# Where the scale sums of the opening are computed: VectorE alone, or GpSimd and ScalarE

## Chip, cores and metric

The kernel runs on one core of a Trainium2 chip. The metric is the time of one execution on the device in microseconds (us), given as the median of several runs. The profile is of one more execution.

## What is computed

The reference is a decoder trunk of two layers on a residual stream x of 512 tokens by 1024 features (D), with a conditioning vector c. Each layer has a SwiGLU channel mixer at half step, a token mixer (retention in layer 0, a diagonal state space in layer 1) and another channel mixer. What matters here is what stands ahead of the first channel mixer:

```
c_act = silu(c)
sh1, sc1, g1, ... = split(c_act @ ada_w[0] + ada_b[0], 9)
h = modulate(rms_norm(x, norm_g[0, 0]), sh1, sc1)      # y * (1 + sc1) + sh1
x = x + 0.5 * g1 * swiglu_ffn(h, ffn_w_in[0, 0], ffn_w_out[0, 0])
```

A shift sh1 or a scale sc1 is a vector of 1024 numbers, and each of them is the inner product of c_act with one column of ada_w. The change is about the scales.

## The kernel before

Features lie on the 128 partitions, so that x is eight tiles of 128 features by 512 tokens (KT = 8). Matrix products with f32 operands are made from two parts: a high part rounded to fp32r (h_hi, w_hi) and the rest (h_lo, w_lo). Each product of a block is three matmuls: h_hi with w_lo, h_hi with w_hi and h_lo with w_hi. ScalarE writes the high parts, VectorE subtracts to get the low parts (the "splits").

The five engines each run an instruction list in order, and wait for each other by semaphores that the program counts by hand. SP and ScalarE's queue issue the loads of the opening: x, the row of c (spread to all partitions in csil), the first pair of weight chunks in halves, and eight blocks ada_first, one for each tile t of features, 1 MB each. A block holds for its 128 features the weights of the shift (index 0) and of the scale (index 1), 1024 each, along the free dimension.

The shift or scale of a tile is thus a sum along the free dimension of the product of such a block with csil. On VectorE one custom instruction makes the product and the sum at once (the function modulation, L1200, and a short one that reads the accumulator); it starts the sum with the bias from par, where the parameters are kept.

In the opening VectorE works as follows. It sums the squares of x, makes the shift and the scale of tile 0 (first_shift, first_scale) and the first halves of the low parts of two weight chunks (split_first, L1423). Then follows a loop over the tiles t (L1400 to L1458): norm_mult (L1400) multiplies x by the scale and by the reciprocal root that TensorE has spread over a bank of PSUM, first_shift makes the shift of tile t + 1, norm_lo (L1405) makes h_lo of tile t, after t = 1 and 2 a second half split follows, and first_scale makes the scale of tile t + 1 (with L1434, which adds 1 and multiplies by the gain of the norm). ScalarE writes h_hi of tile t (L1166) between norm_mult and norm_lo. TensorE (begin, L2339 to L2343) runs twelve matmuls for each tile, eight with h_hi and four with h_lo, into four banks.

GpSimd makes the reciprocal root of the mean square by a power (norm, L642), waits for a small load dt and makes a second power from it, of 128x64 (L688), whose result is read later for the state space layer. Much later it multiplies and adds on six tiles of the state space layer (s5, L670 and L673), counted by the semaphore us_scaled.

Names of the listing: pool is GpSimd, act ScalarE, dve VectorE, sp the queue of loads, pe TensorE; st counts VectorE's own steps, and st.wait() waits until the last of them is written.

Of the kernel before, what the change touches and what calls it, by code (L numbers as in the profile page):

```python
# [10 lines left out]
ALU = mybir.AluOpType  # L11
ACT = mybir.ActivationFunctionType
# [4 lines left out]
KT = D // P  # L17
TT = L // P
# [70 lines left out]
COL_G = 2 * N_MOD * KT  # L89
# [34 lines left out]
def build(nc, ins, out):  # L124
    pos_d = ins["positions"]
    ctx = ExitStack()
    with ctx:
        def sem(name):
            return ctx.enter_context(nc.semaphore(name))
# [30 lines left out]
        mods = sb("mods", [P, 2 * N_MOD * KT])  # L160
        par = sb("par", [P, N_PAR])
        scale1 = sb("scale1", [P, KT])
# [17 lines left out]
        ada_first = sb("ada_first", [P, KT, 2, D], F32, g_at + HB)  # L180
# [35 lines left out]
        csil = sb("csil", [P, D], F32, tz_at)  # L216
# [74 lines left out]
        def st_slot(q, r):  # L291
            slot, count = ST_SLOTS[q, r]
            return slot, IN0 + count
# [47 lines left out]
        tile_in = [sem(f"tile_in{t}") for t in range(KT)]  # L341
        c_row_in, csil_done, mods_ready = sem("c_row_in"), sem("csil_done"), sem("mods_ready")
# [15 lines left out]
        y_last, scaled_act, scaled_dve = sem("y_last"), sem("scaled_act"), sem("scaled_dve")  # L358
# [26 lines left out]
        us_dve, us_pool, us_scaled = sem("us_dve"), sem("us_pool"), sem("us_scaled")  # L385
        consts_e, zeroed, decays_done = sem("consts_e"), sem("zeroed"), sem("decays_done")
        v_done, v_read, sc_done, y_done, gelu_done = sem("v_done"), sem("v_read"), sem("sc_done"), sem("y_done"), sem("gelu_done")
        a5_hi, a5_lo, gate_done = sem("a5_hi"), sem("a5_lo"), sem("gate_done")

        st_in, st_added = [*x_in, *w_first[0]], sem('st_added')  # L390
        t_summed, t_hi_done, t_lo_done = rot_done, rot_hi_done, rot_lo_done
        st_summed, st_hi_done, st_lo_done, st_used = masked, s_hi_done, s_lo_done, score_done
# [17 lines left out]
        def _(sp):  # L410
# [201 lines left out]
            ffn(3)  # L612
            out_v = out.rearrange("b (t p) n -> p (b t) n", p=P)
            for i in range(TT // 2):
                for scaled, t in ((scaled_dve, i), (scaled_act, TT // 2 + i)):
                    sp.wait_ge(scaled, i + 1)
                    sp.dma_start(out_v[:, t], x_tok[:, t]).then_inc(stored, 16)
            sp.wait_ge(stored, 16 * TT)

# [1 line left out]
        @block.gpsimd  # L621
        def _(pool):
            nc.gpsimd.memset(ident[:], 0.0).then_inc(consts, 1)
            nc.gpsimd.memset(ones[:], 1.0).then_inc(consts, 1)
            nc.gpsimd.memset(mhalf[:], -0.5).then_inc(consts, 1)
            nc.gpsimd.memset(ones_d[:], 1.0 / D).then_inc(consts, 1)

            nc.gpsimd.memset(rho[:], float(np.e)).then_inc(consts_e, 1)
            pool.wait_ge(consts, 4)
            nc.gpsimd.affine_select(out=ident[:], in_=ident[:], compare_op=ALU.not_equal, fill=1.0, base=0,  # L630
                                    pattern=[[-1, P]], channel_multiplier=1).then_inc(consts, 1)

            def norm(k):

                if k in EARLY_AT:
                    pool.wait_ge(early_ms, EARLY_AT[k] + 1)
                    nc.gpsimd.tensor_tensor(rstd[:, 0:2], ms[:, 0:2], mhalf[:, 0:2], ALU.pow).then_inc(early_rstd, 1)
                    pool.wait_ge(ms_done, k + 1)
                    nc.gpsimd.tensor_tensor(rstd[:, 2:4], ms[:, 2:4], mhalf[:, 2:4], ALU.pow).then_inc(rstd_done, 1)
                    return  # L640
                pool.wait_ge(ms_done, k + 1)
                nc.gpsimd.tensor_tensor(rstd[:], ms[:], mhalf[:], ALU.pow).then_inc(rstd_done, 1)  # L642

            def retention():
                with pool.Fori(0, HEADS) as h:
                    for I in range(TT):
                        pool.wait_ge(gn_var, h * TT + (I + 1))
                        nc.gpsimd.tensor_tensor(gn[:, I % 2, 1:2], gn[:, I % 2, 0:1], mhalf[:, 0:1],
                                                ALU.pow).then_inc(gn_rstd, 1)
            def s5():  # L650
                pool.wait_ge(params_in, 32)
                pool.wait_ge(mods_done, MODS_NEED[5])
                pool.wait_ge(xn_done, 4 * KT + 2)
                for t in decays:
                    nc.gpsimd.memset(t[:].rearrange("p (g c) -> p g c", c=NC)[:, :, 0:1], 0.0).then_inc(zeroed, 1)
                for t in (*s_prev, zeros):
                    nc.gpsimd.memset(t[:], 0.0).then_inc(zeroed, 1)

                pool.wait_ge(rb_ready, 1)
                for b in range(US_DVE, KT):  # L660

                    if b == US_DVE:
                        pool.wait_ge(v_done, 1)
                    elif b < 6:
                        pool.wait_ge(sc_done, b - 2)
                    else:
                        pool.wait_ge(a5_lo, (1, 3)[b - 6])
                    v = us[:, b].rearrange("p (g c) -> p g c", c=NC)
                    pool.wait_ge(tile_in[b], 32)
                    nc.gpsimd.tensor_tensor(v, v, spread[:].unsqueeze(1).broadcast_to([P, GB, NC]),  # L670
                                            ALU.mult).then_inc(us_scaled, 1)
                    pool.wait_ge(us_scaled, b - US_DVE + 1)
                    nc.gpsimd.tensor_tensor(v, v, us_shift[:, :, b].unsqueeze(2).broadcast_to([P, GB, NC]),  # L673
                                            ALU.add).then_inc(us_pool, 1)

            def add_blocks(f):
                for q in range(FIRST[f], FIRST[f] + BLOCKS[f]):
                    for k, (r, other) in enumerate(((L_S1, A22), (L_S3, A11))):
                        slot, count = st_slot(q, r)
                        pool.wait_ge(st_in[slot], count)  # L680
                        if q or k:
                            pool.wait_ge(st_added, 32 * q + 16 * k)
                        pool.dma_start(st_block(q, r), ins["w_st"][q, other], accum_op=ALU.add).then_inc(st_added, 16)

            norm(0)
            pool.wait_ge(consts_e, 1)
            pool.wait_ge(dt_in, 16)
            nc.gpsimd.tensor_tensor(dt[:], rho[:], dt[:], ALU.pow).then_inc(exp_done, 1)  # L688
            norm(1)
            retention()  # L690
            norm(2)
            add_blocks(1)
            norm(3)
            norm(4)
            s5()
            norm(5)
            add_blocks(3)
            norm(6)
# [3 lines left out]
        def _(act):  # L702
            st = Steps(act, act_steps)
# [454 lines left out]
            for h in range(2):  # L1158
                r = slice(h * HALF, (h + 1) * HALF)
                for k in range(2):  # L1160
                    act.wait_ge(w_first[k][h], 16)
                    copy(w_hi[k][:, r], w_raw[k][:, r]).then_inc((w_hi_half, w_hi_done)[h], 1)
            for t in range(KT):
                act.wait_ge(mods_ready, t + 1)
                act.wait_ge(xn_done, 1 + t + 1)
                nc.scalar.activation(h_hi[:, t], slots[t % 4], ACT.Identity, bias=mods[:, t:t + 1]).then_inc(h_hi_done, 1)  # L1166
            ffn(0)
            retention()
            out_phase(C_RET_OUT, RET_OUT, OUT_PAIRS * 2, begun=True, early=(2, 6 * KT))
# [10 lines left out]
        def _(dve):  # L1180
            st = Steps(dve, dve_steps)
            V = nc.vector
# [225 lines left out]
            def begin():  # L1408
# [17 lines left out]
                def first_shift(t):  # L1426
                    dve.wait_ge(tile_in[t], 16)
                    modulation(ada_first[:, t, 0], slice(t, t + 1)).then_inc(mods_ready, 1)

                def first_scale(t):  # L1430
                    at = slice(KT + t, KT + t + 1)
                    st(modulation(ada_first[:, t, 1], at))
                    st.wait()
                    st(V.scalar_tensor_tensor(out=scale1[:, t:t + 1], in0=mods[:, at], scalar=1.0,  # L1434
                                              in1=par[:, COL_G + t:COL_G + t + 1], op0=ALU.add, op1=ALU.mult))
                    st.wait()
# [4 lines left out]
                dve.wait_ge(stat_done, 1)  # L1441
                V.tensor_scalar(ms[:], ps[:, 4, 0:TT], 1.0 / D, NORM_EPS, ALU.mult, ALU.add).then_inc(ms_done, 1)
                first_scale(0)
                st(V.memset(acc[:], 0.0))
                for k in range(2):
                    split_first(k, 0)
                dve.wait_ge(rbc_done, 1)
                for t in range(KT):
                    if t >= 4:
                        dve.wait_ge(h_lo_done, t - 3)  # L1450
                    norm_mult(t)
                    if t + 1 < KT:
                        first_shift(t + 1)
                    norm_lo(0, t, 0)
                    if t in (1, 2):
                        split_first(t - 1, 1)
                    if t + 1 < KT:
                        first_scale(t + 1)  # L1458
                dve.sem_inc(mods_done, ADA_FIRST)

            def set_coef(l, s, factor, need):
# [1286 lines left out]
US_DVE = 2  # L2748
# [94 lines left out]
```

## Time and profile before

| what | value |
|---|---|
| median of 3 runs | 2075.45 us (2073.07 to 2076.8) |
| the profiled execution: time, span | 2077.54 us, 2075.7 us |
| granted clock of TensorE, mean | 0.995 |
| busy: TensorE, VectorE, ScalarE, GpSimd | 2023.8, 1316.7, 660.1, 69.1 us |

The span is the stretch from the first to the last recorded work of the profiled execution; its own time is a little longer. Busy time is that in which an engine had an instruction in work, waits excluded. All times of the trace are counted from the start of the span, and the opening is about its first 62 us.

### The profile page before, as it was taken

The numbers are of one execution on the slowest core, as the hardware profiler recorded it, in microseconds if no ns is written. First come the engines' busy times: TensorE is split into PE (matmuls) and PEld (weight loads), VectorE is DVE, ScalarE is ACT, GpSimd is POOL, SyncE is SP. The second block draws the span as 40 slices with busy tenths as digits, with TensorE's granted clock in tenths as the row PEclk, the third lists the DMA queues.
The fourth block names the chain that finished last, engine by engine and source line by source line (L and its number), as shares of the span: only waits on it lengthen the run. The fifth ranks groups of instructions, "written<-read, shape, count | busy, mean of one in ns | idle before, by whom it ended". The sixth has DMA issues, their size and how long they took to land.

```text
span 2075.7 us, 27715 instructions
## 1 busy us (share of the span) xinstructions
PE 2023.8 (97%) x11279; PEld 1770.4 (85%) x11279; DVE 1316.7 (63%) x1841; ACT 660.1 (32%) x777; POOL 69.1 (3%) x81
## 2 busy tenths in 40 slices
PE   4999999999999999999999999999998999999998
PEld 3788888998888889888988988888887898999886
DVE  6677556565455466888865566663548757888522
ACT  2322222333232233223432332322232234444322
POOL 2000000000000000000000000000002000100000
PEclk9999999999999999999999999999999999999999
DMA  8455656433233163666666244453797426666421
GB/s 323 142 197 178 204 189 199 162 115 107 81 106 106 61 226 127 215 222 179 167 233 203 89 159 144 144 172 128 236 320 263 128 82 193 183 178 168 153 97 56
DMA packets 233237, 344.04 MB, mean 166 GB/s; under 512 B 33009, under 2 KB 194033, under 8 KB 230257
## 3 DMA queue, kind: packets, MB, share of 16 engines
q1 hardware_dynamic: 195328, 289.95, 41.7%
q10 hardware_dynamic: 34064, 39.07, 5.4%
q0 software_dynamic: 3744, 13.63, 3.9%
q8 instruction: 70, 1.15, 0.2%
q14 instruction: 31, 0.25, 0.0%
HBM read 315.09 MB, written 31.72 MB: 167 GB/s over the span
## 4 chain that ended last, share of the span: by engine, by line
PE 66%; issue 23%; DVE 7%; DMA 1%; ACT 1%; POOL 0%; ACTq 0%; SPq 0%; POOLq 0%; DVEq 0%
PE ps L2166 16%; PE ps L2167 16%; PE ps L2168 16%; PE ps L2193 5%; PE ps L2194 5%; PE ps L2197 5%; DVE ada_first L1200 1%; DVE w_lo L1190 1%; PE ps L2483 1%; DMA w_raw<-in_ffn_w_out 1%; PE ps L2620 0%; DMA csil<-in_c 0%; DVE tur L1721 0%; DVE h_lo L1247 0%; ACT w_hi L704 0%
## 5 line engine op out<-in xcount | busy, mean ns | idle before, releaser
L704 ACT ACTIVATE w_hi<-w_raw 128x1024 fp32r<-128x1024 f32 (+1 forms) x300 | 294.1, 1026 | 344.7 <-PE ps L2168 239.3
L1190 DVE TENSOR_TENSOR w_lo<-w_raw,w_hi 128x1024 fp32r<-128x1024 f32 x146 | 178.5, 1223 | 275.8 <-ACT w_hi L704 270.8
L2166 PE MATMUL ps<-g_hi,w_lo 128*128 128x512 f32 (+1 forms) x952 | 345.9, 363 | 0.2 <-DVE w_lo L1190 0.2
L2168 PE MATMUL ps<-g_hi,w_hi 128*128 128x512 f32 (+1 forms) x952 | 344.9, 362 | 0.0
L2167 PE MATMUL ps<-g_lo,w_hi 128*128 128x512 f32 (+1 forms) x952 | 344.9, 362 | 0.0
L2166 PE MATMUL ps<-h_hi,w_lo 128*128 128x512 f32 x672 | 263.2, 392 | 0.3 <-DVE w_lo L1190 0.3
L2168 PE MATMUL ps<-h_hi,w_hi 128*128 128x512 f32 x672 | 261.8, 390 | 0.0
L2167 PE MATMUL ps<-h_lo,w_hi 128*128 128x512 f32 x672 | 261.7, 389 | 0.0
L2166 PEld LDWEIGHTS ps<-g_hi,w_lo 128*128 128x128 f32 x952 | 179.7, 189 | 28.4 <-DVE w_lo L1190 0.7
L2168 PEld LDWEIGHTS ps<-g_hi,w_hi 128*128 128x128 f32 x952 | 179.7, 189 | 27.9
L2167 PEld LDWEIGHTS ps<-g_lo,w_hi 128*128 128x128 f32 x952 | 179.7, 189 | 27.5
L2193 PE MATMUL ps<-h_hi,w_lo 128*128 128x512 f32 x480 | 188.8, 393 | 2.5 <-DVE w_lo L1190 2.4
L2194 PE MATMUL ps<-h_hi,w_hi 128*128 128x512 f32 x480 | 187.6, 391 | 0.0
L1195 DVE TENSOR_TENSOR w_lo<-w_raw,w_hi 128x1024 fp32r<-128x1024 f32 (+1 forms) x146 | 170.5, 1168 | 0.8 <-DVE acc L1302 0.3
L1200 DVE CUSTOM_DVE_ANT_0 ada_raw<-ada_raw,csil,par 128x1024 f32<-128x1024 f32 x128 | 159.5, 1280 | 7.6 <-DMA ada_raw<-in_ada_w 7.4
L2168 PEld LDWEIGHTS ps<-h_hi,w_hi 128*128 128x128 f32 x672 | 126.2, 188 | 26.5
L2197 PE MATMUL ps<-h_lo,w_hi 128*128 128x512 f32 x480 | 148.6, 391 | 0.0
L2166 PEld LDWEIGHTS ps<-h_hi,w_lo 128*128 128x128 f32 x672 | 126.2, 188 | 26.1 <-issue 0.6
L2167 PEld LDWEIGHTS ps<-h_lo,w_hi 128*128 128x128 f32 x672 | 126.3, 188 | 25.2
L704 ACT ACTIVATE g_hi<-s_buf 128x1024 fp32r<-128x1024 f32 (+1 forms) x35 | 37.1, 1059 | 271.9 <-DVE s_buf L1678 249.8
L2167 PE MATMUL ps<-h_lo,st_whi 128*128 128x256 f32 x416 | 117.7, 283 | 0.0
L2168 PE MATMUL ps<-h_hi,st_whi 128*128 128x256 f32 x416 | 117.7, 283 | 0.0
(317 smaller groups left out, 3562.1 us busy)
## 6 DMA issues: line engine op xcount, KB each, us to landing
ada_raw<-in_ada_w SPq DMA_DIRECT2D x128, 512.0 KB, 4.6
w_raw<-in_ffn_w_in SPq DMA_DIRECT2D x60, 1024.0 KB, 7.1
st_raw<-in_w_st SPq DMA_DIRECT2D x65, 512.0 KB, 4.7
w_raw<-in_ffn_w_out SPq DMA_DIRECT2D x32, 1024.0 KB, 7.1
w_raw<-in_ret_w_in SPq DMA_DIRECT2D x24, 1024.0 KB, 5.3
st_raw<-in_w_st POOLq DMA_DIRECT2D x26, 512.0 KB, 5.4
w_raw<-in_ffn_w_out SPq DMA_DIRECT2D x16, 768.0 KB, 6.6
tb<-s_rec ACTq DMA_DIRECT2D x8, 1536.0 KB, 7.6
```

The source lines that it names most:

```text
L704: copy = lambda o, i: nc.scalar.activation(o, i, ACT.Copy)
L1190: V.tensor_tensor(w_lo[k % 2][:, 0:HALF, :], w_raw[k % 2][:, 0:HALF, :], raw_f32(w_hi[k % 2][:, 0:HALF, :]), ALU.subtract).then_inc(w_lo_h ...
L1195: V.tensor_tensor(w_lo[k % 2][:, HALF:r, :], w_raw[k % 2][:, HALF:r, :], raw_f32(w_hi[k % 2][:, HALF:r, :]), ALU.subtract).then_inc(w_lo_d ...
L1200: return V.tensor_tensor_reduce(out=raw, in0=raw, in1=csil[:], scale=1.0, scalar=par[:, at], op0=ALU.mult, op1=ALU.add, accum_out=mods[:, at])
L2166: nc.tensor.matmul(o, wl, xh, start=start, stop=False)
L2167: nc.tensor.matmul(o, wh, xl, start=False, stop=False)
L2168: return nc.tensor.matmul(o, wh, xh, start=False, stop=stop)
L2193: nc.tensor.matmul(ps[:, bank + c], wl[c], h_hi[:, t], start=t == 0, stop=False)
L2194: nc.tensor.matmul(ps[:, bank + c], wh[c], h_hi[:, t], start=False, stop=False)
L2197: m = nc.tensor.matmul(ps[:, bank + c], wh[c], h_lo[:, t], start=False, stop=t == KT - 1)
L2483: m = nc.tensor.matmul(ps[:, 6, g * SK:(g + 1) * SK], ys[:, g, 0:SC, :].rearrange("p d k -> p (d k)"), xs[:, g, SC - 1], start=True, stop= ...
```

## The change

For tiles 1 to 7 the scale sum is taken from VectorE. GpSimd multiplies the scale block of the tile in place by csil, after its first power and ahead of the second. ScalarE copies the product in place and lets its accumulator sum it into mods: the sum of tile 1 after h_hi of tile 0, and the sum of tile t + 2 after h_hi of tile t. VectorE waits for that sum and makes of it, in one small instruction, the scale with the gain; one small instruction ahead adds 1 to the biases of all seven tiles, which before were the start of the sum. Tile 0, the shifts, the loads, the squares and the splits stay. Two semaphores are used a second time (us_scaled for the products, scaled_act for the sums), so that later waits on them count seven more.

```
+        scale_product, scale_summed = us_scaled, scaled_act
...
-                for scaled, t in ((scaled_dve, i), (scaled_act, TT // 2 + i)):
-                    sp.wait_ge(scaled, i + 1)
+                for scaled, n, t in ((scaled_dve, 0, i), (scaled_act, KT - 1, TT // 2 + i)):
+                    sp.wait_ge(scaled, n + i + 1)
...
-                    pool.wait_ge(us_scaled, b - US_DVE + 1)
+                    pool.wait_ge(us_scaled, KT - 1 + b - US_DVE + 1)
...
             norm(0)
+            pool.wait_ge(csil_done, 1)
+            for t in range(1, KT):
+                pool.wait_ge(tile_in[t], 16)
+                nc.gpsimd.tensor_tensor(ada_first[:, t, 1], ada_first[:, t, 1], csil[:], ALU.mult).then_inc(scale_product, 1)
             pool.wait_ge(consts_e, 1)
             pool.wait_ge(dt_in, 16)
             nc.gpsimd.tensor_tensor(dt[:], rho[:], dt[:], ALU.pow).then_inc(exp_done, 1)
...
+            def sum_scale(t):
+                act.wait_ge(scale_product, t)
+                nc.scalar.activation(ada_first[:, t, 1], ada_first[:, t, 1], ACT.Copy,
+                                     accum_out=mods[:, KT + t:KT + t + 1]).then_inc(scale_summed, 1)
+
             for t in range(KT):
                 act.wait_ge(mods_ready, t + 1)
                 act.wait_ge(xn_done, 1 + t + 1)
                 nc.scalar.activation(h_hi[:, t], slots[t % 4], ACT.Identity, bias=mods[:, t:t + 1]).then_inc(h_hi_done, 1)
+                if t == 0:
+                    sum_scale(1)
+                if t + 2 < KT:
+                    sum_scale(t + 2)
...
+                def scale_of(t):
+                    dve.wait_ge(scale_summed, t)
+                    st.wait()
+                    st(V.scalar_tensor_tensor(out=scale1[:, t:t + 1], in0=mods[:, KT + t:KT + t + 1], scalar=scale1[:, t:t + 1],
+                                              in1=par[:, COL_G + t:COL_G + t + 1], op0=ALU.add, op1=ALU.mult))
+                    st.wait()
...
                 first_scale(0)
+                st(V.tensor_scalar(scale1[:, 1:KT], par[:, KT + 1:2 * KT], 1.0, None, ALU.add))
                 st(V.memset(acc[:], 0.0))
...
                     if t + 1 < KT:
-                        first_scale(t + 1)
+                        scale_of(t + 1)
```

## Rows read from the trace of the kernel before

**Rows 1.** Busy time by stretch: bounds, length, engines, granted clock, DMA share, GB/s.
```profile
44.00:48.00 4.00, 4.00 (x11) 2.79 (x10) 3.93 (x8) 0.72 (x1) 4.00 (x1) 0.57 0.65 258
...
52.00:56.00 4.00, 2.99 (x14) 2.12 (x13) 3.93 (x8) 0.72 (x1) 0.00 (x0) 1.00 0.01 4
```

**Rows 2.** Chain of waits, end of the opening: start us, us, what.
```profile
57.95 0.73 ACT h_hi L1166
...
59.22 0.23 PE ps L2340
```

**Rows 3.** Timeline of VectorE: start us, us, line, operation, tiles, shapes.
```profile
24.14 2.29 DVE L1423 TENSOR_TENSOR w_lo<-w_raw,w_hi 128x1024 fp32r<-128x1024 f32 x2
26.41 0.75 DVE L1400 SCALAR_TENSOR_TENSOR s_buf<-x_sb,scale,ps 128x512 f32<-128x512 f32 x1
27.08 1.28 DVE L1200 CUSTOM_DVE_ANT_0 ada_first<-ada_first,csil,par 128x1024 f32<-128x1024 f32 x1
...
28.28 0.75 DVE L1405 SCALAR_TENSOR_TENSOR h_lo<-s_buf,mods,h_hi 128x512 fp32r<-128x512 f32 x1
28.95 1.28 DVE L1200 CUSTOM_DVE_ANT_0 ada_first<-ada_first,csil,par 128x1024 f32<-128x1024 f32 x1
...
30.27 0.16 DVE L1434 SCALAR_TENSOR_TENSOR scale<-mods,par 128x1 f32<-128x1 f32 x1
30.47 0.75 DVE L1400 SCALAR_TENSOR_TENSOR s_buf<-x_sb,scale,ps 128x512 f32<-128x512 f32 x1
...
57.10 0.75 DVE L1400 SCALAR_TENSOR_TENSOR sq<-x_sb,scale,ps 128x512 f32<-128x512 f32 x1
```

**Rows 4.** Timeline of TensorE in the opening.
```profile
28.69 0.63 PE L2340 MATMUL ps<-h_hi,w_hi 128*128 128x512 f32 x1
29.12 0.63 PE L2339 MATMUL ps<-h_hi,w_lo 128*128 128x512 f32 x1
...
33.81 0.40 PE L2340 MATMUL ps<-h_hi,w_hi 128*128 128x512 f32 x1
...
61.14 0.61 PE L2343 MATMUL ps<-h_lo,w_hi 128*128 128x512 f32 x2
```

**Rows 5.** Page, busy time and share of the span by engine.
```profile
PE 2023.8 (97%) x11279; PEld 1770.4 (85%) x11279; DVE 1316.7 (63%) x1841; ACT 660.1 (32%) x777; POOL 69.1 (3%) x81
```

**Rows 6.** Page, groups of instructions: count, busy us, mean ns, idle before.
```profile
L704 ACT ACTIVATE g_hi<-s_buf 128x1024 fp32r<-128x1024 f32 (+1 forms) x35 | 37.1, 1059 | 271.9 <-DVE s_buf L1678 249.8
```

**Rows 7.** Timeline of GpSimd in the state space layer.
```profile
1573.16 1.06 POOL L673 TENSOR_TENSOR moving<-moving,us_shift 128x512 f32<-128x512 f32 x1
...
1579.04 1.27 POOL L670 TENSOR_TENSOR moving<-moving,spread 128x512 f32<-128x512 f32 x1 [4.82 <-DVEq L2081]
1580.39 1.92 POOL L673 TENSOR_TENSOR moving<-moving,us_shift 128x512 f32<-128x512 f32 x1
```

**Rows 8.** VectorE there, and the line's durations in ns: least, median, largest.
```profile
1573.22 0.69 DVE L1721 TENSOR_TENSOR rot<-ps,tb 128x512 f32<-128x512 f32 x1
...
1579.05 2.34 DVE L1195 TENSOR_TENSOR w_lo<-w_raw,w_hi 128x1024 fp32r<-128x1024 f32 x1
...
L1195 DVE TENSOR_TENSOR w_lo<-w_raw,w_hi x146: 683/1218/2339, 63.6 to 2046.3; 128x1024 fp32r<-128x1024 f32 x130, 128x512 fp32r<-128x512 f32 x16
```

**Rows 9.** Timelines of GpSimd's powers, and of VectorE beside the large one.
```profile
22.25 1.99 POOL L642 TENSOR_TENSOR rstd<-ms,mhalf 128x4 f32<-128x4 f32 x1 [20.65 <-DVE ms L1442]
38.90 10.92 POOL L688 TENSOR_TENSOR dt<-rho,dt 128x64 f32<-128x64 f32 x1 [14.66 <-DMA dt<-in_s_log_dt]
...
2066.86 1.03 POOL L642 TENSOR_TENSOR rstd<-ms,mhalf 128x4 f32<-128x4 f32 x1 [161.10 <-DVE ms L1385]
...
39.32 1.35 DVE L1200 CUSTOM_DVE_ANT_0 ada_first<-ada_first,csil,par 128x1024 f32<-128x1024 f32 x1
```

**Rows 10.** Timeline of VectorE, first reader of the large power's result.
```profile
72.85 0.36 DVE L1721 TENSOR_TENSOR sm<-sm,dt 128x64 f32<-128x64 f32 x2
```

**Rows 11.** Page, loads by line: count, size, median us to landing.
```profile
w_raw<-in_ffn_w_in SPq DMA_DIRECT2D x60, 1024.0 KB, 7.1
```

## Prediction

> **What bounds the kernel now.** I read the stretches first. In the opening VectorE is busy 3.93 of every 4 us, ScalarE 0.72, GpSimd nothing from 52 to 56 (from 44 to 48 it runs a power that nobody waits for yet), and TensorE, where its granted clock is 1.00, has a quarter of the time to spare [rows 1]. The chain of waits agrees: through the opening it runs along VectorE's instructions and leaves them only after tile 7, by ScalarE's h_hi to TensorE [rows 2]. VectorE's timeline gives one tile's step [rows 3]: normalising product 0.67 (26.41 to 27.08), shift sum 1.20 (to 28.28), h_lo 0.67 (to 28.95), scale sum with its small instructions 1.52 (to 30.47); 4.06 in all. The reader should see that each begins where the one ahead ends. Seven such steps and two more half splits (1.15 each, half of the pair at 24.14) take it from 26.41 to 57.10. TensorE's matmuls follow each other every 0.43 us in the first tiles, until 33.81 [rows 4], and every 0.23 at the end [rows 2]: its two clocks, 1.2 and 2.4 GHz. From 44 to 48 the granted clock was 0.57, the low one for most of it [rows 1]. Twelve matmuls make a tile: 2.75 us at the high clock, 5.1 at the low one. The last two start at 61.14 and 0.23 later and end near 61.6 [rows 4]. TensorE is busy 97% of the whole span [rows 5], so what the opening gains or loses I carry to the end one to one.
>
> **What is removed.** Tiles 1 to 7 lose the VectorE scale sum. Its 1.52 becomes one 128x1 instruction whose slot is 0.20 (30.27 to 30.47) [rows 3]: 7 x 1.32 = 9.24 us less. Added once ahead of the splits is a small tensor_scalar, 0.20 by the same slot. The new step would be 0.67 + 1.20 + 0.67 + 0.20 = 2.74 us.
>
> **What is added on ScalarE.** Each tile there now costs 0.72, for h_hi [rows 1], plus a copy of 128x1024, 1.06 by the mean row of such copies [rows 6]. The read of its accumulator is not in the trace: at least nothing, at most 0.3 (a quarter of the copy). At most 2.1 us a tile, under 2.74, so I take nothing. Behind a waiting copy the next h_hi is queued, and TensorE behind that: it matters only if a product is late. VectorE's new wait holds its normalising product back; by the walk below the sum of tile 1 is ready near 32 and the slot of its scale is past 37.
>
> **What is added on GpSimd.** Seven products 128x1024, f32, both inputs in SBUF. The nearest rows are 128x512 on the same engine: 1.27 for a product, 1.06 for a sum [rows 7]. Twice the elements: between 2.1 and 2.5; the product row is nearer. GpSimd is free from 24.24, when its first power ends, and the tiles come in time: the small load of dt, issued behind all of them on SP's queue, is in at 38.90 [rows 9], and the last two products come after 40 (below).
>
> **The cost that decides: the second input.** At 1579.05 VectorE's 128x1024 subtraction of two SBUF tiles took 2.34 instead of a median of 1.22 (the largest of 146) while GpSimd's product ran from 1579.04 to 1580.31; and GpSimd's next instruction, begun at 1580.39 beside the rest of that subtraction, took 1.92 instead of 1.06 [rows 7, 8]. So one waited for the whole of the other, both ways: VectorE lost 1.12 to a product of 1.27, GpSimd 0.86. A VectorE product of PSUM and one SBUF tile, at 1573.22, ran 0.69 beside a GpSimd sum that took its usual 1.06: no hold there. The opening has the same two kinds: shift sum, h_lo, splits and the small scale instruction read two SBUF tiles; the normalising product reads one and PSUM. GpSimd's first power at 22.25 took 1.99 against 1.03 at the end of the kernel: it may have stood for one of VectorE's sums. The large power ready at 38.90 got in between two VectorE instructions that follow each other, with 0.07 more on the second of them (1.35 against 1.28) [rows 3, 9]. I therefore let the engines take turns. One product holds VectorE for 2 x 1.12 = 2.24; by the sum's row, 2 x 0.92 = 1.84 (1.06 less the same 0.14).
>
> The walk: product 1 comes between the two half splits at 25.3 (2.24 lost); product 2 starts with the first normalising product, which hides 0.67 (1.57 lost); product 3 between shift 1 and h_lo 0 (2.24); product 4 between h_lo 0 and the scale of tile 1 (2.24); product 5 beside that tile's normalising product (1.57); product 6 between shift 2 and h_lo 1; product 7 between h_lo 1 and the split (2.24 each). By then it is about 46, so no landing is waited for. Lost: 5 x 2.24 + 2 x 1.57 = 14.34. All products lie in the first three tiles; from there VectorE steps in 2.74.
>
> VectorE net: 14.34 + 0.20 - 9.24 = +5.3 us; its last normalising product moves from 57.10 to 62.4. With 1.84 it is 5 x 1.84 + 2 x 1.17 + 0.20 - 9.24 = +2.5; with nothing hidden and 2.24 it is +6.6.
>
> **TensorE behind it.** Its 2.75 now equals VectorE's 2.74, so what it once falls behind it does not make up. The steps of tiles 0 to 2 are some 9 us apart, so I expect the low clock where the dense tiles begin: tile 2 takes 5.1 there against a step of 3.9 (2.74 and a split): 1.2 behind. If the clock is high, nothing. I take half, +0.6. Sum: +5.9.
>
> **Moved.** GpSimd's large power (10.92) waited for its data until 38.90; now it starts after product 7, near 46, and ends near 57. VectorE reads its result at 72.85 now [rows 10], some 6 later in the new kernel: 15 us of cover or more. The loads of the second weight pair wait for the second half splits, then near 47 and 51; such a load lands 7.1 later [rows 11], and the pair is wanted after tile 7, past 62. Behind them on SP's queue stand only later loads. The copies into the output at the very end wait for a count raised by seven: nothing.
>
> **A rule weighed.** The small power row shows GpSimd waiting, but during the 10.92 us of the large one VectorE's two-input sum at 39.32 ran in 1.35 [rows 9]; the hold there was 0.07, not 10.9. The Trainium skill, SBUF — State Buffer, section "Who interferes with whom", says that whoever issues first gets the shared pair for the whole instruction and the other fully blocks. By that rule the power at 46 would stop VectorE once more, where now its second input was free. For products the rule and the row at 1579 agree; for the power the trace contradicts it. By the rule the sum would be 5.9 + 10.9 = +17, by the row +5.9, and I go by the row.
>
> **Rivals.**
> - Taking turns, as above (chance 0.56): +5.9, with its own range +2.5 to +8.
> - VectorE keeps its second input through instructions that follow each other, and products run only beside the normalising products and in gaps (0.10): each loses 2.24 - 0.67 = 1.57; 7 x 1.57 + 0.20 - 9.24 = +2. For it: nothing shows GpSimd breaking in except the 0.07 at 39.32.
> - GpSimd keeps it through products that stand back to back (0.12): 7 x 2.24 from 25.3 on, none hidden: 15.7 + 0.2 - 9.24 = +6.6, with TensorE's share +7 to +9.5. Against it: at 1580.31 VectorE came ahead of GpSimd's next instruction, though GpSimd waited 0.08 for itself there.
> - The other side, no hold (0.14): the sum type of instruction, a custom one, or plain contiguous products could run side by side. Then VectorE's last product comes 9.0 earlier, at 48.1. TensorE decides: from its second matmul at 28.69, 12 of 0.43 and 83 of 0.23 give 52.9 instead of 61.6, so -8.7 us. It decides wherever a product costs VectorE under about 1.3 us (9.04 / 7). Against it: the one row where both read two tiles, and the wait at 22.25.
> - The power holds VectorE throughout (0.03): 10.9 more, +17. Against it: the row at 39.32.
> - Something else late, between -3 and +4 (0.05).
>
> **The numbers.** The profiled execution took 2077.54 (span 2075.7 and 1.84 around it), 2.1 above the median of 2075.45. +5.9 on its own time is 2083.4; against the median, 2081.3. The cases: 2081.3, 2077.5, 2082 to 2085, 2066.8, 2092. The range 2072 to 2085.5 leaves out the case without a hold, the power's and the tails, about 0.2; the likeliest case's own is 2078 to 2083.5. A change of 0.2% is 4.15 us, about what these runs can tell from none. Taking turns passes it in about three quarters of its range (0.41), a GpSimd that keeps its turn nearly always (0.11), the power always (0.03), with 0.01 of the rest: slower 0.56. Same: 0.15 + 0.10 + 0.01 + 0.03 = 0.29. Faster: 0.15, the case without a hold and the rest of the last.
>
> **What would show it.** Right: in the new opening the VectorE instructions beside GpSimd's products take 1.2 + 2.2 or 0.7 + 2.2 us, products stretched by VectorE's in turn, all seven done near 46; steps of 2.7 afterwards, low granted clock at tile 2 or 3, the last opening matmul near 67. Wrong: shift sums at 1.28 beside products (then 53), or products only beside normalising products (then 64), or all seven in one row from 25 to 41. It is wrong too if a product takes far from 2.4 us, if ScalarE's copy with its accumulator takes more than 2, or if TensorE's idle stretches after the opening change.

## The result: 0.29% slower, and the profile after

| | before | after |
|---|---|---|
| median | 2076.01 us (7 runs, 2072.73 to 2077.29) | 2080.93 us (7 runs, 2079.57 to 2083.43) |
| ratio | | 1.0029, 95% interval 1.002 to 1.0039 |
| profiled execution: span | 2075.7 us | 2079.9 us |
| mean granted clock | 0.995 | 0.992 |

The medians differ by 4.9 us; the ratio, 1.0029, would be 6.0 us, and its interval, 4.2 to 8.1 us, holds both. The opening accounts for it: the first matmul of the second weight pair starts at 63.70 before and at 68.27 after (further below), 4.57 later, and from there to the end the two profiled executions take nearly the same, 2012.0 and 2011.6 us. The line before:

```profile
63.70 0.50 PE L2193 MATMUL ps<-h_hi,w_lo 128*128 128x512 f32 x1 [1.94 <-DVE w_lo L1190]
```

VectorE's timeline of the new opening, to be laid beside [rows 3] (start us, us, line, operation, tiles):

```profile
24.10 4.44 DVE L1438 TENSOR_TENSOR w_lo<-w_raw,w_hi 128x1024 fp32r<-128x1024 f32 x2
28.46 0.73 DVE L1415 SCALAR_TENSOR_TENSOR s_buf<-x_sb,scale,ps 128x512 f32<-128x512 f32 x1
29.12 2.72 DVE L1215 CUSTOM_DVE_ANT_0 ada_first<-ada_first,csil,par 128x1024 f32<-128x1024 f32 x1
...
31.76 2.84 DVE L1420 SCALAR_TENSOR_TENSOR h_lo<-s_buf,mods,h_hi 128x512 fp32r<-128x512 f32 x1
34.53 2.32 DVE L1448 SCALAR_TENSOR_TENSOR scale<-mods,scale,par 128x1 f32<-128x1 f32 x1
36.88 0.75 DVE L1415 SCALAR_TENSOR_TENSOR s_buf<-x_sb,scale,ps 128x512 f32<-128x512 f32 x1
37.55 2.68 DVE L1215 CUSTOM_DVE_ANT_0 ada_first<-ada_first,csil,par 128x1024 f32<-128x1024 f32 x1
...
40.16 2.84 DVE L1420 SCALAR_TENSOR_TENSOR h_lo<-s_buf,mods,h_hi 128x512 fp32r<-128x512 f32 x1
42.93 3.38 DVE L1438 TENSOR_TENSOR w_lo<-w_raw,w_hi 128x1024 fp32r<-128x1024 f32 x1
46.23 0.27 DVE L1448 SCALAR_TENSOR_TENSOR scale<-mods,scale,par 128x1 f32<-128x1 f32 x1
...
47.20 1.28 DVE L1215 CUSTOM_DVE_ANT_0 ada_first<-ada_first,csil,par 128x1024 f32<-128x1024 f32 x1
...
58.80 0.75 DVE L1415 SCALAR_TENSOR_TENSOR sq<-x_sb,scale,ps 128x512 f32<-128x512 f32 x1
...
61.58 0.75 DVE L1415 SCALAR_TENSOR_TENSOR sq<-x_sb,scale,ps 128x512 f32<-128x512 f32 x1
```

The reader should see that seven durations are too long, each by most of a product of GpSimd. The pair of splits takes 4.44 instead of 2.29; the shift sums 2.72 and 2.68 instead of 1.28, h_lo twice 2.84 instead of 0.75, the third split 3.38 instead of 1.22. Plainest is the scale instruction: one number for each partition, 2.32 us instead of 0.16 (0.21 in its new form where nothing hinders it, at 58.55). The sum is 2.15 + 1.44 + 2.09 + 2.16 + 1.40 + 2.09 + 2.16 = 13.49 us. The normalising products, which read x and PSUM, take 0.75 as before in the middle of all this. The splits and h_lo share no tile with the products, so a tile in common is not the reason. From 46 on everything has its old duration, and a step is 2.78 (58.80 to 61.58).

GpSimd's side: its first and last product in the timeline, the spread of all seven (least, median, largest ns; first and last start), and the power behind them.

```profile
24.10 3.36 POOL L690 TENSOR_TENSOR ada_first<-ada_first,csil 128x1024 f32<-128x1024 f32 x1
...
42.41 2.81 POOL L690 TENSOR_TENSOR ada_first<-ada_first,csil 128x1024 f32<-128x1024 f32 x1
...
L690 POOL TENSOR_TENSOR ada_first<-ada_first,csil x7: 2354/3330/3357, 24.1 to 42.4; 128x1024 f32<-128x1024 f32 x7
...
45.19 11.53 POOL L693 TENSOR_TENSOR dt<-rho,dt 128x64 f32<-128x64 f32 x1
```

A product unhindered takes 2.35; the median of 3.33 has a VectorE instruction of about a microsecond in it. During the power VectorE's shift sum at 47.20 runs in 1.28.

ScalarE's copy with its sum, which the trace before could not show:

```profile
38.35 1.04 ACT L1171 ACTIVATE ada_first<-ada_first 128x1024 f32<-128x1024 f32 x1
39.30 0.19 ACT L1171 ACTIVATION_READ_ACCUMULATOR ada_first<-ada_first 128x1 f32 x1
```

TensorE around tile 2 and after the opening, beside [rows 4]:

```profile
48.15 0.79 PE L2362 MATMUL ps<-h_hi,w_lo 128*128 128x512 f32 x1 [3.02 <-ACT h_hi L1177]
48.74 0.63 PE L2363 MATMUL ps<-h_hi,w_hi 128*128 128x512 f32 x1
49.17 0.63 PE L2362 MATMUL ps<-h_hi,w_lo 128*128 128x512 f32 x1
...
51.60 1.08 PE L2366 MATMUL ps<-h_lo,w_hi 128*128 128x512 f32 x4
52.53 0.39 PE L2362 MATMUL ps<-h_hi,w_lo 128*128 128x512 f32 x1
52.76 0.40 PE L2363 MATMUL ps<-h_hi,w_hi 128*128 128x512 f32 x1
...
63.43 0.39 PE L2362 MATMUL ps<-h_hi,w_lo 128*128 128x512 f32 x1
...
68.27 0.62 PE L2216 MATMUL ps<-h_hi,w_lo 128*128 128x512 f32 x1 [1.96 <-DVE w_lo L1205]
```

And the stretches (columns as in [rows 1]):

```profile
44.00:48.00 4.00, 1.13 (x3) 0.33 (x1) 3.96 (x4) 0.62 (x1) 4.00 (x2) 0.50 0.08 13
48.00:52.00 4.00, 3.85 (x10) 3.08 (x11) 3.96 (x7) 1.84 (x5) 4.00 (x1) 0.57 0.82 267
52.00:56.00 4.00, 4.00 (x19) 3.26 (x19) 3.94 (x9) 2.82 (x6) 4.00 (x1) 1.00 1.06 372
```

TensorE starves from 44 to 48 (1.13 of 4 us), its granted clock is the low one there and for most of the next stretch (0.43 between matmuls), and high from 52 on (0.23). VectorE is busy throughout by the record: its waits for GpSimd are inside its durations, and no view of waits names them.

### The profile page after: what moved, and what is told of

Same layout as the page of the kernel before. It is cut to its first block, busy times and chain, and to the rows that moved or that the text cites. A ratio compares the mean times of both kernels' runs of the same rounds, so it can differ in the third digit from the quotient of the medians.

```text
span 2079.9 us, 27731 instructions
## 1 busy us (share of the span) xinstructions
PE 2024.3 (97%) x11279; PEld 1771.6 (85%) x11279; DVE 1321.8 (64%) x1828; ACT 667.5 (32%) x791; POOL 90.6 (4%) x88
## 4 chain that ended last, share of the span: by engine, by line
PE 69%; issue 23%; DVE 5%; DMA 1%; ACT 1%; POOL 0%; ACTq 0%; POOLq 0%; SPq 0%; DVEq 0%
PE ps L2189 17%; PE ps L2191 17%; PE ps L2190 17%; PE ps L2216 5%; PE ps L2217 5%; PE ps L2220 5%; PE ps L2506 1%; PE ps L2643 0%; DMA csil<-in_c 0%; DVE tur L1744 0%; DVE h_lo L1262 0%; DVE rot L1744 0%; DVE w_lo L1205 0%; DVE w_lo L1438 0%; PE ps L2497 0%
```

## Experiments

**1. The change without its products.** ScalarE sums the blocks as loaded.

```
-            for t in range(1, KT):
-                pool.wait_ge(tile_in[t], 16)
-                nc.gpsimd.tensor_tensor(ada_first[:, t, 1], ada_first[:, t, 1], csil[:], ALU.mult).then_inc(scale_product, 1)
...
-                act.wait_ge(scale_product, t)
+                act.wait_ge(tile_in[t], 16)
```

> The changed kernel without its seven products: ScalarE sums the blocks as they were loaded, so the scales are not those of the reference; all else stays. Theory (each product holds VectorE's second input by turns, some 13.5 us in all): VectorE loses nothing, its step is 2.8 us from the first tile on, its last normalising product comes near 48.5, TensorE sets the end of the opening near 53, and the time is some 8.5 us below that of the kernel before the change (2067 to 2069). Rival (the loss lies in the way of a scale over ScalarE's accumulator and two more waits, not in the products): the time stays near that of the changed kernel, above the kernel before.

Measured: 2066.05 against 2074.83, ratio 0.9959 (0.9944 to 0.9975): -8.8 us. VectorE's last normalising product, and TensorE's first matmul after the opening:

```profile
47.81 0.75 DVE L1411 SCALAR_TENSOR_TENSOR sq<-x_sb,scale,ps 128x512 f32<-128x512 f32 x1
```
```profile
54.40 0.50 PE L2212 MATMUL ps<-h_hi,w_lo 128*128 128x512 f32 x1 [1.96 <-DVE w_lo L1201]
```

So the way over ScalarE by itself, with no product to wait for, costs nothing. The whole loss, and the loss of a gain of some 9 us, lies in GpSimd's products. From the one line to the other it is 6.59, as before (57.10 to 63.70, 6.60): VectorE still sets the end here, where the expectation had TensorE.

**2. Products alone.** The kernel before, and on GpSimd seven products into a spare buffer; later waits on their count are raised by seven, and ScalarE waits for all seven before the work behind the opening.

```
             norm(0)
+            pool.wait_ge(csil_done, 1)
+            for t in range(1, KT):
+                spare = squares[:, 2 * (t % 4):2 * (t % 4) + 2].rearrange("p a n -> p (a n)")
+                pool.wait_ge(tile_in[t], 16)
+                if t > 4:
+                    pool.wait_ge(us_scaled, 1 * (t - 4))
+                nc.gpsimd.tensor_tensor(spare, csil[:], csil[:], ALU.mult).then_inc(us_scaled, 1)
```

> The kernel before with seven products of csil by csil on GpSimd at the place of the changed kernel's, into a buffer that nobody reads; VectorE still makes every scale sum. Theory (turns): by the changed kernel's rows a product costs VectorE 2.15 us, or 1.45 where it starts with a normalising product; in the old order of instructions that is five of the first kind and two of the second, +13.7 us, plus 0 to 1 for TensorE's clock: 2089 to 2091. Rival (no hold; the loss is in the handing over): 0 us, 2076.

Measured: 2085.7, ratio 1.0053 (1.0037 to 1.0068): +10.9 us. The direction is the theory's, the size is not: about 3 us short. The spread of the products shows why, and one h_lo beside them:

```profile
L692 POOL TENSOR_TENSOR squares<-csil x7: 1887/2865/2871, 24.1 to 39.5; 128x1024 f32<-128x1024 f32 x7
```
```profile
30.77 2.37 DVE L1413 SCALAR_TENSOR_TENSOR h_lo<-s_buf,mods,h_hi 128x512 fp32r<-128x512 f32 x1
```

A product of csil by itself takes 1.89 unhindered, not 2.35, and h_lo lost 1.62 (2.37 less 0.75), not 2.09. The experiment had changed the size of what it wanted to hold fixed; run 5 repairs it.

**3. GpSimd writes, and reads nothing.** As run 2, with two memsets for each product.

```
-                nc.gpsimd.tensor_tensor(spare, csil[:], csil[:], ALU.mult).then_inc(us_scaled, 1)
+                for k in range(2):
+                    if k:
+                        pool.wait_ge(us_scaled, 2 * t - 1)
+                    nc.gpsimd.memset(spare, 0.0).then_inc(us_scaled, 1)
```

```profile
24.17 5.77 POOL L695 MEMSET squares<- 128x1024 f32 x6
```
```profile
27.05 1.28 DVE L1211 CUSTOM_DVE_ANT_0 ada_first<-ada_first,csil,par 128x1024 f32<-128x1024 f32 x1
```

Writing 128x1024 tiles holds nobody. Nor does long computing: beside the power of 11.53 us in the changed kernel the shift sum at 47.20 took 1.28. What is left is GpSimd's reading of its inputs.

**4. The row in PSUM.** The changed kernel, with csil copied to two free banks for the shift sums.

```
+            copy(ps[:, 6:8, :].rearrange("p a n -> p (a n)"), csil[:]).then_inc(csil_done, 1)
...
-                    modulation(ada_first[:, t, 0], slice(t, t + 1)).then_inc(mods_ready, 1)
+                    modulation(ada_first[:, t, 0], slice(t, t + 1), ps[:, 6:8, :].rearrange("p a n -> p (a n)")).then_inc(mods_ready, 1)
```

> The changed kernel with the row csil copied to two free banks of PSUM by ScalarE, from where VectorE's eight shift sums read it; they then read one SBUF tile. Products, splits, h_lo and the small scale instruction stay. Theory (only two SBUF inputs are held): shift sums run at about 1.3 us beside products; products hold h_lo, the splits and the scale instruction alone. By the walk the last normalising product comes near 58.6, 3 us ahead of the changed kernel and 1.5 after the kernel before: about 2078. Rival (a VectorE instruction is held whatever its inputs): as the changed kernel, 2081.

Measured: 2076.92, ratio to the kernel before 1.001 (1.0001 to 1.0019): +2.1 us against +4.9 of the change. In its trace the opening ends 0.8 later than before (64.52 against 63.70). VectorE's timeline:

```profile
29.40 1.27 DVE L1217 CUSTOM_DVE_ANT_0 ada_first<-ada_first,ps,par 128x1024 f32<-128x1024 f32 x1
...
31.52 2.33 DVE L1450 SCALAR_TENSOR_TENSOR scale<-mods,scale,par 128x1 f32<-128x1 f32 x1
...
36.66 3.40 DVE L1440 TENSOR_TENSOR w_lo<-w_raw,w_hi 128x1024 fp32r<-128x1024 f32 x1
39.99 2.29 DVE L1450 SCALAR_TENSOR_TENSOR scale<-mods,scale,par 128x1 f32<-128x1 f32 x1
...
57.66 0.75 DVE L1417 SCALAR_TENSOR_TENSOR sq<-x_sb,scale,ps 128x512 f32<-128x512 f32 x1
```

The sum beside a product is back at 1.27, now that its second input comes from PSUM; the split and the small scale instruction, still with two SBUF inputs, wait as before. The last normalising product comes at 57.66 where the walk had 58.6.

**5. Products alone, of two tiles.** Run 2 with x in place of one csil.

```
-                nc.gpsimd.tensor_tensor(spare, csil[:], csil[:], ALU.mult).then_inc(us_scaled, 1)
+                nc.gpsimd.tensor_tensor(spare, x_sb[:, 0:2].rearrange("p a n -> p (a n)"), csil[:], ALU.mult).then_inc(us_scaled, 1)
```

> As the run with products alone, but each product is of two different tiles (x and csil) in place of csil by itself. In that run a product of csil by itself took 1.89 us unhindered and held VectorE 1.6 to 1.7, against 2.35 and 2.15 in the changed kernel. Theory (the hold is as long as GpSimd reads, and two different inputs are read as in the changed kernel): 2.35 us unhindered, five times 2.15 and twice 1.45 lost, +13.7 us and 0 to 1 for TensorE: 2088 to 2090. Rival (something else in the changed kernel made its products long): as in that run, +11.

Measured: 2088.32 against 2075.26, ratio 1.0063 (1.0047 to 1.0079): +13.1 us, where 13.7 to 14.7 was expected.

```profile
L692 POOL TENSOR_TENSOR squares<-x_sb,csil x7: 2347/3315/3347, 23.7 to 41.9; 128x1024 f32<-128x1024 f32 x7
```
```profile
31.32 2.84 DVE L1413 SCALAR_TENSOR_TENSOR h_lo<-s_buf,mods,h_hi 128x512 fp32r<-128x512 f32 x1
```

Duration and hold are those of the changed kernel (2.35, and 2.09 lost by h_lo). The products alone cost 13.1; the change takes 9 off VectorE and nets 4.9.

**6. Control: the row in PSUM, nothing on GpSimd.** The same edit as run 4 on the kernel before.

> Control: the kernel before with nothing but the row csil copied to PSUM and read from there by the shift sums. No product on GpSimd, so nothing to be freed. Theory: 0 us within 1 (the sums ran 1.27 from PSUM and 1.28 from SBUF; the copy lies in ScalarE's idle time). Rival (the gain of the run with the row in PSUM came from the PSUM input itself): 2 to 4 us faster than before.

Measured: 2076.1, ratio 1.0002 (0.9992 to 1.0011): no difference clear of the noise. The gain of run 4 is not PSUM's own.

**7. Out of the way.** Run 4, with the half splits ahead of the products and the scale instruction without its second SBUF input.

```
+            pool.wait_ge(w_lo_done, 3)
             for t in range(1, KT):
...
                 for k in range(2):
                     split_first(k, 0)
+                for k in range(2):
+                    split_first(k, 1)
...
-                    if t in (1, 2):
-                        split_first(t - 1, 1)
...
-                    st(V.scalar_tensor_tensor(out=scale1[:, t:t + 1], in0=mods[:, KT + t:KT + t + 1], scalar=scale1[:, t:t + 1],
-                                              in1=par[:, COL_G + t:COL_G + t + 1], op0=ALU.add, op1=ALU.mult))
+                    st(V.tensor_scalar(scale1[:, t:t + 1], mods[:, KT + t:KT + t + 1], scale1[:, t:t + 1],
+                                       par[:, COL_G + t:COL_G + t + 1], ALU.add, ALU.mult))
```

> The run with the row in PSUM, and two more steps out of GpSimd's way: all four half splits stand ahead of the first normalising product and the first product waits for them, and the small scale instruction takes its gain as a pointer scalar in place of a second SBUF input. Only h_lo (0.67 a tile) still reads two SBUF tiles beside products. Theory: a step is at most 3.1 us while products last, VectorE's last normalising product comes near 52, TensorE (its start 2.3 us later by the splits) ends near 56.6 against 61.6: 5 us below the kernel before, 2071. Rival (the path over ScalarE and GpSimd is too long, so that each tile waits for its sum): steps near 4 us, no gain over the kernel before.

Measured: 2068.58, ratio 0.9963 (0.9949 to 0.9977): -6.7 us.

```profile
24.05 4.56 DVE L1441 TENSOR_TENSOR w_lo<-w_raw,w_hi 128x1024 fp32r<-128x1024 f32 x4
...
30.39 1.27 DVE L1423 SCALAR_TENSOR_TENSOR h_lo<-s_buf,mods,h_hi 128x512 fp32r<-128x512 f32 x1
...
32.33 0.27 DVE L1451 TENSOR_SCALAR scale<-mods,scale,par 128x1 f32<-128x1 f32 x1 [0.67 <-ACT ada_first L1174]
...
35.72 1.06 DVE L1423 SCALAR_TENSOR_TENSOR h_lo<-s_buf,mods,h_hi 128x512 fp32r<-128x512 f32 x1 [1.14 <-ACT h_hi L1180]
...
51.17 0.75 DVE L1418 SCALAR_TENSOR_TENSOR sq<-x_sb,scale,ps 128x512 f32<-128x512 f32 x1
```

Of the durations only those of h_lo in tiles 0 and 1 still grow a little (0.52 and 0.31); from there each h_lo fits between two products. The scale instruction with its pointer scalar takes 0.27 beside a product: it is not held.

In the first two tiles the theory's step of at most 3.1 us missed: by the starts of the normalising products (28.53, 32.63, 37.01) they took 4.10 and 4.38. There the rival is right, though the gain stands. VectorE waits 0.67 for the sum of tile 1 (at 32.33) and 1.14 for h_hi of tile 1 (at 35.72), which stood on ScalarE behind the sum of tile 2, and that sum waited 1.63 for its product. From 37.01 on a step is 2.83.

**8. The first product early.** Run 7, with the product of tile 1 ahead of GpSimd's first power, and tile 0's scale sum reading PSUM too.

```
-            norm(0)
             pool.wait_ge(csil_done, 1)
-            pool.wait_ge(w_lo_done, 3)
             for t in range(1, KT):
+                if t == 2:
+                    norm(0)
+                    pool.wait_ge(w_lo_done, 3)
```

> As the run out of the way, and the product of tile 1, in since 19.7, stands ahead of GpSimd's first power; the scale sum of tile 0 reads the row from PSUM too. Theory: that product runs from 19.8 to 22.1 beside one-input work and costs nothing, GpSimd is one product ahead, TensorE's own work sets the end: near 55 against 61.6, 6.5 below the kernel before, 2069.5. Rival (it holds up VectorE's sum of squares at 19.2 and the power): 0.5 to 1 us later than the run out of the way.

Measured: 2067.36, ratio 0.9961 (0.9947 to 0.9975): -7.9 us. GpSimd's timeline, and TensorE's first matmul after the opening:

```profile
19.38 2.53 POOL L692 TENSOR_TENSOR ada_first<-ada_first,csil 128x1024 f32<-128x1024 f32 x1 [17.79 <-DMA ada_first<-in_ada_first]
22.01 1.03 POOL L643 TENSOR_TENSOR rstd<-ms,mhalf 128x4 f32<-128x4 f32 x1
```
```profile
56.50 0.50 PE L2220 MATMUL ps<-h_hi,w_lo 128*128 128x512 f32 x1 [1.96 <-DVE w_lo L1209]
```

Runs 7 and 8 beat both kernels. That 8 beats 7 their intervals don't show; in the two traces the opening of run 8 ends 1.26 earlier (57.76 in run 7), and its first two steps are 3.30 and 2.83 instead of 4.10 and 4.38. TensorE sets the end there, as expected: from the last normalising product (48.75) to that matmul it is 7.75, where the kernel before has 6.60. The power now takes 1.03 where it took 1.99 in [rows 9]: with the sum beside it reading PSUM, it no longer waits. So the wait of [rows 9] was for one of VectorE's sums, as the prediction supposed.

## Why the prediction was right

The change was forecast at +5.9 us and measured at +4.9 by the medians (+6.0 by the ratio), by the way of the likeliest case. Its terms were off by 0.85 (the hold, too large), 0.3 (the new slot, too small) and 0.5 (TensorE, too large); that the second offsets a part of the others is luck. Together they leave 4.85, where the opening in the traces has 4.57. By its own steps:

- **What bounds the kernel.** Right. The opening's 4.57 us arrive at the end nearly whole (4.2 in the spans, 4.9 in the medians).
- **What is removed.** 9.24 right but for the new small instruction: the step is 2.78 (58.80 to 61.58), not 2.74, so its slot is nearer 0.25 than 0.20; 0.3 in seven tiles. The instruction added once took 0.22, forecast 0.20.
- **ScalarE.** 1.04 and 0.19 to read the accumulator, inside the bounds of nothing and 0.3, and hidden. Run 1 shows it.
- **A product's duration.** 2.35, between the bounds of 2.1 and 2.5.
- **The hold.** Right in kind: two SBUF inputs on VectorE and a reading GpSimd take turns. Shown by run 1 (no products, -8.8), run 3 (no reading, no loss) and run 4 (no second SBUF input, no wait), with run 6 as control. The size was 2.24 from a 128x512 row doubled; measured 2.09 to 2.16, and 1.40 to 1.44 where a normalising product hides part, against 1.57. So 13.49 was lost instead of 14.34: the term that was mis-sized.
- **The walk.** The places of the seven products were all as forecast, the last one done at 45.2 against "near 46". The last normalising product came at 61.58, forecast 62.4: 13.49 - 9.24 + 0.3 = +4.55, and from the first split, behind the instruction added once, to that product the traces have 37.48 against 32.96, +4.52.
- **TensorE behind it.** The low clock at tile 2 came as forecast, the cost did not. Only eight of the tile's twelve matmuls ran at the low clock (until 51.60), so it took 4.38 (48.15 to 52.53) and not 5.1, and tile 3 started 0.5 late, when its h_hi was already there. VectorE's step of 2.78 is slower than TensorE's 2.72 to 2.74 a tile (it starts tiles 3, 4 and 5 at 52.53, 55.27 and 57.99), so by tile 7 the delay was 0.3 (h_hi there at 63.14, first matmul at 63.43). The matmuls of tile 7 followed without a pause ahead of them, and from the first start to the last they took 2.50 instead of 2.65. From the last normalising product to the first matmul after the opening it is 6.69 after and 6.60 before: 0.1, where 0.6 was taken.
- **The rule of the whole instruction.** The Trainium skill, SBUF — State Buffer, section "Who interferes with whom", also says that a VectorE instruction with two SBUF inputs contends with a GpSimd instruction that reads SBUF and not with one that only writes; runs 3 and 4 agree (a sum took 1.28 beside memsets, and 1.27 beside a product with one input in PSUM). Its lock for the whole instruction holds nearly so for the products (2.09 to 2.16 of their 2.35) and not for the power of 11.5 us, beside which a two-input sum took 1.28.
- **The rivals.** VectorE keeping its input would have put products beside normalising products alone; GpSimd keeping it, all seven in a row. The timeline shows neither. No hold is excluded by run 5, the power's hold by the sum at 47.20 (1.28).

## What to carry to other kernels

A product moved from VectorE to GpSimd may take nothing off VectorE if VectorE meanwhile runs instructions with two SBUF inputs: price it at nearly its full duration on both engines (here 2.35 on GpSimd and some 2.1 on VectorE, against 1.32 saved), less what one-input work hides. Look first whether one operand can be read from PSUM or, as shown here for a 128x1 instruction, as a pointer scalar; here that and a better place for the products turned +4.9 us into -6.7 and -7.9. Such a hold doesn't show as idle time: look for durations that are longer than the same shape's elsewhere, the shortest instruction first. What does show as idle time is a product that comes late: in run 7 the first two kept VectorE waiting, the second by way of ScalarE's queue.

## What was not expected of the hardware

GpSimd's product of a tile by itself took 1.89 us and held VectorE 1.6, its product of two tiles 2.35 and 2.1, at the same 128x1024 f32. Why is open: no run varies the inputs further.
